# A new order of small steps in a hybrid decoder layer: convolution taps, pool products, MoBA's early units, a transfer and two fills

## The reference, cut to what matters

```python
z = x @ w_in
# A convolution: GLU, depthwise width 31, LayerNorm, swish, pointwise
z_ = a * sigmoid(g); y = conv(z_, dw) + dw_b
y_conv = silu(layer_norm(y)) @ pw
# B sparse attention (NSA): compressed blocks, top-16 selected blocks, window
hid = chunks @ w1 + bias; kc, vc = silu(hid) @ w2
p = masked_softmax(q @ kc); imp = p.sum(heads) @ cover; idx = top_k(imp, 16)
o_nsa = gates . (p @ vc, softmax(q @ ks[idx]) @ vs[idx], softmax(q @ k_win) @ v_win)
# C MoBA: blocks of 256 keys, top 3 by q . mean(k), plus the own block
o_moba = softmax(q @ k[idx]) @ v[idx]
# D pooling: trailing means over 2/4/8/16 rows minus the row, a map per group
y_pool = ((means - rows) @ pool_w) * pool_scale
x = LN(alpha * x + concat(y_conv, o_nsa, o_moba, y_pool) @ w_out)
x = LN(alpha * x + relu(x @ w_up)**2 @ w_down)
```

## Time and profile before

| | |
|---|---|
| median of 3 runs | 762.71 us |
| the profiled execution | 759.45 us |
| its span in the profile | 757.8 us |
| mean granted TensorE clock | 0.998 |
| PE busy | 734.4 us (97%) |
| DVE, ACT, POOL busy | 429.3, 284.9, 210.2 us |

### The profile page before, as it was taken

The page is one execution under the profiler, slowest core; times in us unless marked ns, Lnnn a source line. Parts: engine busy times, 40 slices in busy tenths (PEclk is TensorE's granted clock), DMA queues, the critical chain, the costliest instruction groups (busy, mean ns, idle before and its releaser), DMA issues.

```text
span 757.8 us, 17347 instructions
## 1 busy us (share of the span) xinstructions
PE 734.4 (97%) x6904; PEld 657.6 (87%) x6904; DVE 429.3 (57%) x741; ACT 284.9 (38%) x559; POOL 210.2 (28%) x284
## 2 busy tenths in 40 slices
PE   9999999799999899999999999999999999999997
PEld 8999988687665455599999999999999999999996
DVE  4878994646665543358765566334553345536365
ACT  5222334345665222524534444112431233323125
POOL 0000576013336760006457611001110011100433
PEclk9999999999999999999999999999999999999999
DMA  9656799585888942431432232332333222325002
GB/s 336 184 156 176 204 296 284 213 296 175 278 303 301 299 127 90 142 112 56 174 106 84 84 111 89 116 104 73 96 98 97 84 85 84 112 84 168 1 15 101
DMA packets 63980, 113.49 MB, mean 150 GB/s; under 512 B 17017, under 2 KB 36218, under 8 KB 63226
## 3 DMA queue, kind: packets, MB, share of 16 engines
q1 hardware_dynamic: 57370, 95.58, 39.7%
q0 software_dynamic: 6528, 16.78, 6.4%
HBM read 107.90 MB, written 6.52 MB: 151 GB/s over the span
## 4 chain that ended last, share of the span: by engine, by line
PE 80%; DVE 7%; issue 4%; SPq 4%; ACT 3%; DMA 1%; POOL 0%; ACTq 0%; DVEq 0%
PE psum L849 57%; PE psum L868 4%; PE psum L876 4%; PE psum L924 2%; SPq L759 2%; PE psum L1152 2%; PE psum L989 2%; PE psum L955 1%; PE psum L1140 1%; DMA wgate<-in_w_gate 1%; DVE wL L1690 1%; PE psum L1188 1%; DVE oxL L2119 1%; PE psum L1205 1%; PE psum L1092 1%
## 5 line engine op out<-in xcount | busy, mean ns | idle before, releaser
L1690 DVE TENSOR_TENSOR wL<-raw,wH 128x1024 fp32r<-128x1024 f32 (+1 forms) x85 | 107.1, 1261 | 87.2 <-ACT wH L1313 87.2
L1313 ACT ACTIVATE wH<-raw 128x1024 fp32r<-128x1024 f32 (+1 forms) x87 | 88.8, 1021 | 103.0 <-PE psum L849 100.6
L849 PE MATMUL psum<-oxH,wH 128*128 128x260 f32 (+1 forms) x512 | 105.0, 286 | 0.7 <-DVE oxL L2119 0.5
L849 PE MATMUL psum<-oxH,wL 128*128 128x260 f32 (+1 forms) x512 | 103.9, 284 | 0.0
L849 PE MATMUL psum<-oxL,wH 128*128 128x260 f32 (+1 forms) x512 | 103.4, 283 | 0.0
L1652 POOL TENSOR_TENSOR hsq<-relu 128x520 f32<-128x520 f32 x32 | 33.8, 1055 | 217.9 <-ACT relu L1493 217.9
L849 PE MATMUL psum<-opH,wH 128*128 128x260 f32 x400 | 85.8, 296 | 2.5 <-DVE wL L1690 1.4
L849 PEld LDWEIGHTS psum<-oxH,wH 128*128 128x128 f32 x512 | 79.5, 189 | 2.5 <-issue 1.7
L849 PE MATMUL psum<-opH,wL 128*128 128x260 f32 x400 | 80.3, 282 | 0.0
L849 PE MATMUL psum<-opL,wH 128*128 128x260 f32 x400 | 80.3, 282 | 0.0
L849 PEld LDWEIGHTS psum<-oxL,wH 128*128 128x128 f32 x512 | 79.9, 190 | 0.0
(11 more groups left out here) (418 smaller groups left out, 1311.1 us busy)
## 6 DMA issues: line engine op xcount, KB each, us to landing
raw<-in_panels SPq DMA_DIRECT2D x88, 512.0 KB, 3.5
nsa_ring<-in_nsa_pages SPq DMA_DIRECT2D x128, 96.0 KB, 2.3
moba_hi<-in_moba_pages SPq DMA_DIRECT2D x24, 256.0 KB, 5.2
moba_lo<-in_moba_pages SPq DMA_DIRECT2D x24, 256.0 KB, 4.2
moba_hole<-in_moba_pages SPq DMA_DIRECT2D x16, 256.0 KB, 4.8
moba_hi<-in_moba_pages POOLq DMA_DIRECT2D x16, 256.0 KB, 5.8
moba_lo<-in_moba_pages POOLq DMA_DIRECT2D x16, 256.0 KB, 5.4
moba_ring<-in_moba_pages POOLq DMA_DIRECT2D x12, 256.0 KB, 5.3
```

Source lines behind the costliest of these rows:

```text
L849: last = mm(out[:, hf, 0:cols], w, x[:, k, hf * HALF:hf * HALF + cols], start=(t == 0 and j == 0), stop=(t == KT - 1 and j == 2))
L1313: fn(wtiles(0, n).rearrange("p a b -> p (a b)")[:, cols], raw[:, n % NRAW, cols], ACT.Copy).then_inc(h_done, 1)
L1690: tt(wtiles(1, n).rearrange("p a b -> p (a b)")[:, cols], raw[:, n % NRAW, cols], wtiles(0, n).rearrange("p a b -> p (a b)")[:, cols].bitc ...
```

## The change

It is the order of steps in TL, with two pieces of code cut out of a step to stand as steps of their own (`selx`, the exp of the last sample's Psel, and `clears`, the two fills). The number of instructions of each kind stays the same. Lines of the changed kernel are 2 higher up to L1350 and 5 higher behind.

- Taps: 1 behind panel 1 and 4 behind panel 2, for 6 and 6; 8, 8, 9, 9 behind panels 3 to 6, for 6, 6, 7, 8.
- Behind panel 10: pool(0) and qm stand ahead of nsa(5), for behind it.
- Second early pair: pool(1) stands right behind mu(1), ahead of nsa(7); mt(1) and mp(1) stand behind the first and second piece of panel 13, for on either side of pool(1); selx stands behind cpw.
- Smaller: mp(2) one piece later, mp(4) one row later, mu(11) ahead of lse, for three pieces behind it.
- Behind the last panel: mu, mt, mp of pair 12 later by two steps of the attention, mu(13) and mu(14) a step earlier, the fills behind stat(4), load_winV behind the load of unit 15's pages, mpv and finm some steps later.

```diff
-TAPS_BEHIND = {1: 6, 2: 6, 3: 6, 4: 6, 5: 7, 6: 8, 7: 8, 8: 8, 9: 7}
+TAPS_BEHIND = {1: 1, 2: 4, 3: 8, 4: 8, 5: 9, 6: 9, 7: 8, 8: 8, 9: 7}
...
         if i == ATT_PANEL:
...
-            return (out + m[:1] + [("kv", B)] + m[1:2] + [("mu", 2)] + m[2:4] + [("csc", 0), ("mt", 2)] + m[4:5] + [("zcols", 0), ("mp", 2)] + m[5:6]
-                    + r[:1] + m[6:7] + r[1:2] + m[7:8] + [("evac", i)] + extras + r[2:])
+            return (out + m[:1] + [("mt", 1), ("kv", B)] + m[1:2] + [("mp", 1), ("mu", 2)] + m[2:4] + [("csc", 0), ("mt", 2)] + m[4:5] + [("zcols", 0)] + m[5:6]
+                    + [("mp", 2)] + r[:1] + m[6:7] + r[1:2] + m[7:8] + [("evac", i)] + extras + r[2:])
         if i == N_IN_PANELS - 1:
...
-            return (out + spread(atoms, extras) + [("lse", 0)] + rest[:3] + [("mu", MB1 - 1)] + rest[3:]
+            return (out + spread(atoms, extras) + [("mu", MB1 - 1), ("lse", 0)] + rest
...
-                      11: out, 12: [("mt", 4)], 13: [("mp", 4)], 15: [("cimp", 0)], 16: [("mu", 5)], 17: [("evac", i)], 18: [("mt", 5)]}
+                      11: out, 12: [("mt", 4)], 14: [("mp", 4)], 15: [("cimp", 0)], 16: [("mu", 5)], 17: [("evac", i)], 18: [("mt", 5)]}
...
+            if i == 10:
+                step += [("pool", 0), ("qm", 0)]
             if i == 12:
-                step.append(("mu", 1))
+                step += [("mu", 1), ("pool", 1)]
...
         if i == 10:
-            tl += [("pool", 0), ("cmean", 0), ("pdiff", 1), ("qm", 0), ("out_conv", 0)]
+            tl += [("cmean", 0), ("pdiff", 1), ("out_conv", 0)]
...
         if i == 12:
-            tl += [("mt", 1), ("pool", 1), ("mp", 1), ("cpw", 0), ("cpw", 1), ("load_lo", 0)]
+            tl += [("cpw", 0), ("cpw", 1), ("selx", 0), ("load_lo", 0)]
...
-    units = [(1.5, ("load_winV", 0))]
+    units = [(15, ("load_winV", 0)), (16.2, ("clears", 0))]
     for g in range(MB1, MB):
-        at_ = 1 + PAIR_T * (g - MB1)
-        units += [(at_, ("mu", g)), (at_ + 2.5, ("mt", g)), (at_ + 4.7, ("mp", g))]
+        at_ = 0.9 + PAIR_T * (g - MB1)
+        units += [(at_, ("mu", g)), (at_ + 2.5, ("mt", g)), (at_ + 4.7, ("mp", g))] if g > MB1 else [(3.3, ("mu", g)), (5.9, ("mt", g)), (7.9, ("mp", g))]
...
-    last = [(join_, ("statm", 0)), (join_ + 0.1, ("combm", 0)), (join_ + 6.5, ("combe", 1)), (join_ + 8, ("combm", 1)), (join_ + 9.5, ("combm", 2)), (join_ + 12, ("backm", 0)), (join_ + 15.5, ("mpv", 0)),
-            (join_ + 19, ("finm", 0)), (end + 8, ("msplit", 6)), (end + 25, ("msplit", 7))]
+    last = [(join_, ("statm", 0)), (join_ + 0.1, ("combm", 0)), (join_ + 6.5, ("combe", 1)), (join_ + 8, ("combm", 1)), (join_ + 9.5, ("combm", 2)), (join_ + 12, ("backm", 0)), (join_ + 17, ("mpv", 0)),
+            (join_ + 20.5, ("finm", 0)), (end + 8, ("msplit", 6)), (end + 25, ("msplit", 7))]
...
-                    if kind == "nsa":
+                    if kind == "nsa" and n < B - 1:
                         act.wait_ge(ssel_sub, n + 1)
                         fn(Psel[:, n, :], Psel[:, n, :], ACT.Exp).then_inc(ssel_exp, 1)
+                elif kind == "selx":
+                    act.wait_ge(ssel_sub, B)
+                    fn(Psel[:, B - 1, :], Psel[:, B - 1, :], ACT.Exp).then_inc(ssel_exp, 1)
...
-                    if n == 2:
-                        nc.vector.memset(WB[:, :, :], 0.0)
-                        chain(nc.vector.memset(gdiag[:, :, :], 0.0))
+                elif kind == "clears":
+                    nc.vector.memset(WB[:, :, :], 0.0)
+                    chain(nc.vector.memset(gdiag[:, :, :], 0.0))
```

## The result

The changed kernel took 766.04 us as the median of six runs (762.23 to 767.43), for 762.68 of the kernel before (759.81 to 763.18): ratio 1.0044, 95% interval 1.0023 to 1.0065. It is 3.4 us slower; I had forecast 762.1. The profiled execution took 767.41 us, with a span of 765.7 and a mean granted clock of 0.986, for 757.8 and 0.998 before.

What follows compares the result with a forecast made beforehand. PE bounds the kernel (busy 734.4 of 757.8 us), so only its waits count. Parts of -1.1, +0.6, -0.3, -0.4, -0.7, -0.6 sum to -2.5; clock +1.9 makes -0.6 on 762.71: 762.1 us, range 760.0 to 764.0.

Steps and rivals of the forecast that it cites:

- Taps: Panels 3 to 8: PE's 1.41 us wait at panel 3 goes, 0.34 returns at panel 8; -1.1 us.
- Behind panel 10: First unit, panel 11: waits of 1.08 and 1.14 go, pages cost about 1.1, QM lengthens DVE's chain; +0.6 us.
- Second early pair: Around nsa(7) and panel 13: waits of 3.65 and 0.75 replace 4.6 us of waits and half clock; -0.3 us.
- The clock: Falls to half clock behind the pool(1) wait and unit 15's page wait, 0.95 us each; +1.9 us.
- Smaller ones: mp(2) a piece later removes PTm's 0.39 wait, -0.4 us; MoBA's sum waits about 0.75, -0.7 us.
- Behind the last panel: Late units: waits of 3.0 us in sum go, one of 3.5 stands ahead of unit 15's scores; -0.6 us.
- My -2.5: Sum in us of all forecast parts at full clock, before adding 1.9 for two more clock falls.
- rival B: No clock fall, 760.2 us, or one with QM's copies quick, 760.3 us; chance 0.13.
- QM at 0.7: Behind panel 10: the four copies to QM take 0.7 us, making that part -1.2; the forecast took 2.5.
- Rival C: winV beside unit 15's pages delays the last page to 6.8 us landing; +1.9 us, 764.6 us; chance 0.14.

Runs made afterwards that it cites:

- e1: The kernel before with only the change's new numbers of taps; 760.12 us, ratio 0.9976 to the kernel before.
- e2: The kernel before with only pool(0) and qm moved ahead of nsa(5); 766.21 us, ratio 1.0062 to the kernel before.
- f1: The changed kernel with the four copies to QM made by ACT in place of DVE; 762.04 us, ratio 0.9985 to the kernel before.
- f2: The changed kernel with pool(1) back behind nsa(7), mt(1) and mp(1) left in panel 13; 764.68 us, ratio 1.0024 to the kernel before.
- f4: The changed kernel with 48 unread 128x128 matmuls added in front of its three long waits; 761.58 us, ratio 0.9980 to the kernel before.
- i1: The changed kernel with the second half of each pair's selV loads behind the next unit's pages; 761.16 us, ratio 0.9977 to the kernel before.
- e3: The kernel before with only the second early pair's part of the change; 763.59 us, ratio 1.0016 to the kernel before.
- h1: The kernel before with new taps, early pool(0), QM by ACT, new orders at panel 11 and second early pair, mp(2), mpv, finm; 756.56 us, ratio 0.9911.
- h3: The kernel before with h1's changes plus mu(11), the fills and later selV loads, but winV as before; 752.65 us, ratio 0.9866 to the kernel before.

## Why the prediction was wrong

Where a part begins and ends is read from places in PE's timeline: mt(0), mu(1), the third piece of panel 13, and mp(4). The last row is the landing of unit 15's last page (issue, us to landing). The kernel before:

```profile
120.23 0.27 PE L1147 MATMUL psum<-cst,Pm 128*128 128x128 f32 x1
...
136.98 0.64 PE L1140 MATMUL psum<-moba_v,QM 128*32 128x128 f32 x16 [0.53 <-DMA moba_ring<-in_moba_pages]
...
156.58 0.51 PE L849 MATMUL psum<-opH,wH 128*128 128x260 f32 x2
...
191.02 0.64 PE L1152 MATMUL psum<-moba_hole,PTm 128*32 128x256 f32 x8 [0.85 <-DVE PTm L1876]
...
263.71 4.03 DMA moba_lo<-in_moba_pages
```

The changed kernel (its mt(0) at 123.24 and its mu(1) at 139.64 are shown above):

```profile
161.62 0.51 PE L851 MATMUL psum<-opH,wH 128*128 128x260 f32 x2
...
190.78 0.19 PE L1114 MATMUL psum<-cst,ps_small 127*8 127x33 f32 x1 [0.60 <-issue]
...
196.09 0.64 PE L1154 MATMUL psum<-moba_hole,PTm 128*32 128x256 f32 x8 [0.84 <-DVE PTm L1881]
```

**Taps (-1.1): right.** No wait at panel 3, 0.17 given back at panel 8 for 0.34; PE is 1.4 earlier there. e1 by itself gives 1.8 [0.8, 3.0].

**Behind panel 10 (+0.6): this step failed.** I had said that QM's four copies lie on DVE's chain, and sized them well (2.22 for 2.5). But I followed that chain to the maxima and the transpose of the first unit only, and let the scores wait for pages, 1.1. That wait was not there: the pages had landed by 112.2, where I had put 113.9 or later. (The moba_v of the earlier trace rows are pages of the second early pair, not values of the first unit; its scores wait for them all the same, since one semaphore counts all twelve transfers.) The scores write bank 0, which belongs to pair 0, and the last user of pair 0 was the convolution's mean, whose reader is L1809: `bank(0, step)` in the step's code waits for it. That was in the code, and no row of before showed it, as L1809 ended at 113.69 and the scores came at 116.25. The place cost 4.13 in place of 1.08, 1.14, and a fall of the clock that I had nowhere in my sum: mt(0) came 3.0 later than before, so against the taps' -1.4 the part is +4.4, for +0.6. The clock's share can be read by itself: from the scores to mt(0) the same matmuls took 6.78 us (116.46 to 123.24) for 3.98 (116.25 to 120.23), 2.8 more. e2 shows that the part does this without the taps, f1 that the wait and the fall go with DVE's copies.

**Second early pair (-0.3, clock apart): the waits right, 3.98 and 0.84 for 3.65 and 0.75.** What it came to was not: in the profile the scores of this pair came 2.7 us later than before, and the third piece of panel 13, behind all of it, 5.0 later, so the part is +2.4 for -0.3 + 0.95.

**The clock (+1.9): falls right at two places, missed at the third, and each too cheap.** I took the length of the one fall of before, 3.4 us, as that of any. All three were of 6.8 us in this profile; f2's has three of 3.4 behind waits as long, so that neither length is a rule. The price of the one of before I had as 1.3: from the value products through both halves of cpw its rows are 6.0 us (146.95 to 152.95) for 4.4 at full clock (1.00 and 3.42), 1.6. PE's busy time grew by 4.7, so the three cost 6.3 in sum, some 2 each, for 0.95. f4 gives 5.6 by its busy time and 4.9 by its ratio for the three places.

**Smaller ones: right.** mp(2) took its 0.39 away, MoBA's sum waits 0.76 for 1.47. mp(4) I had left out of the sum: its wait is 0.84 for 0.85, and a new one of 0.60 stands ahead of it (L1114).

**Behind the last panel (-0.6): mis-sized.** The wait of 3.55 was forecast at 3.5, and that SyncE's queue is the bound is shown by i1. But unit 15's scores came 1.0 later than the place before them by the profile (6.1 later than before, against 5.1 at mp(4)) in place of 0.6 earlier: the last page was issued 5.0 later than before (268.7 for 263.7), about as much later as PE was, so that winV's slot of 0.9 brought nothing; and it took 5.1 to land for 4.0. Where the slot went is not shown in full; SyncE issued unit 14's four pages in 3.12 us for 1.93.

**The sum.** My -2.5 counts the 1.3 of before's fall as given back. Put like for like, the waits were forecast at -1.2 and measured at +3.2, the clock at +0.6 (1.9 less 1.3) and measured at +4.7. Three slips of arithmetic stand beside that: 4.4 for 4.6 is -0.2 and not -0.3; the waits that the change touches are some 13 us by my own list and not 11; and in rival B one fall with QM at 0.7 gives 759.4, below my range (760.3 is that case with two falls). None of them explains the 3.9 us by which the forecast was low. My range ended at 764.0, reaching into C; it held no case in which the scores of the first unit are late, which is what went wrong. That I counted one fall of the clock too few came from the same omission. Rival C (764.6) pointed the right way, but not for what happened: it decides from a landing of 6.2 on, and the page took 5.1.

## What to carry to other kernels

When a step is moved behind or ahead of another, go through every wait in its code, also those for a buffer's last reader, and compute when each would end after the move: the trace names only the one that ended last; another had ended 2.6 us before it here, and became the bound. Price a long wait twice, once as idle time and once by the clock that may fall behind it. Whether several short waits are better than one long one is not shown: e3, which made one of two, can't be told from no change, and the two of 1.55 and 1.73 had a fall behind them as well. An engine that is idle (ACT here, 38% busy) is the place for small copies that stand in a busy one's queue. Where a late page is the bound, look at what stands ahead of it in the queue that issues it: one number there gave 5.1 us (i1).

## What was unexpected in the hardware

Waits of 3.6 to 4.1 us in the changed kernel's profile each had 6.8 us at 1.2 GHz in and behind them, some 2 us of work more; matmuls whose result no one reads, placed in the waits, took that away and made the kernel 4.9 us quicker. No length of wait decides by itself in these profiles: 1.78 (e1), 1.96 and 2.02 (h1) had 3.4 us at 1.2 GHz behind them, while 2.24 in the changed kernel, 2.53 in f1 (both for unit 14's pages) and the same 2.02 in h3 had none. A VectorE operation on 128x8 elements took 1.52 us beside POOL's adds (L1773 above), where its twin took 0.24 in the kernel before, in which these adds began only later (110.7 us).
